# VectorE takes over the weight and token sums of a seven-product matmul

## The reference, cut to what matters

```python
x = x + gate1 * mix
h2 = rmsnorm(x, norm2_g) * (1.0 + scale2) + shift2
ffn = (jax.nn.silu(h2 @ w_ffn_gate) * (h2 @ w_ffn_up)) @ w_ffn_down
x = x + gate2 * ffn
```

## Time and profile before

| what | value |
|---|---|
| median of 3 runs | 1331.96 us (1331.69 to 1333.9) |
| the profiled execution's own time | 1333.38 us |
| its span in the profile | 1331.7 us |
| TensorE busy (matmul) | 1269.5 us, 95% |
| VectorE busy | 801.0 us, 60% |
| ScalarE busy | 488.4 us, 37% |
| GpSimd busy | 313.5 us, 24% |
| TensorE's granted clock, mean | 0.99 |

### The profile page before, as it was taken

The page is one execution under the profiler, slowest core; times in us unless marked ns, Lnnn a source line. Parts: engine busy times, 40 slices in busy tenths (PEclk is TensorE's granted clock), DMA queues, the critical chain, the costliest instruction groups (busy, mean ns, idle before and its releaser), DMA issues.

```text
span 1331.7 us, 19817 instructions
## 1 busy us (share of the span) xinstructions
PE 1269.5 (95%) x7734; PEld 1159.1 (87%) x7734; DVE 801.0 (60%) x1308; ACT 488.4 (37%) x812; POOL 313.5 (24%) x273
## 2 busy tenths in 40 slices
PE   5999999999999999998999899997999999999997
PEld 2798887799999999987788798887998899889986
DVE  4553112467566634372899654477873888558866
ACT  5352323353321222223677422344441344313434
POOL 1011000311011011111899400026400443005300
PEclk9999999999999999999899999999999999999999
DMA  9634231154344343452000224211323133222221
GB/s 312 193 111 119 63 95 48 40 159 142 112 158 148 122 110 98 128 187 94 1 1 2 81 79 174 64 32 32 95 95 95 32 95 96 95 63 63 88 88 79
DMA packets 87392, 129.56 MB, mean 97 GB/s; under 512 B 3529, under 2 KB 64450, under 8 KB 87186
## 3 DMA queue, kind: packets, MB, share of 16 engines
q1 hardware_dynamic: 76880, 95.17, 22.6%
q0 software_dynamic: 9104, 32.20, 7.9%
q10 hardware_dynamic: 1330, 1.10, 0.2%
HBM read 117.43 MB, written 4.73 MB: 92 GB/s over the span
## 4 chain that ended last, share of the span: by engine, by line
PE 74%; DVE 11%; POOL 6%; ACT 4%; issue 3%; DMA 1%; ACTq 0%; DVEq 0%
PE psum L421 30%; PE psum L458 27%; PE psum L664 10%; DVE seven_lo L694 5%; POOL probs L961 3%; POOL probs L967 3%; PE psum L407 1%; DVE hid L2158 1%; PE psum L1036 1%; PE psum L522 1%; PE psum L594 1%; DVE w_lo L390 1%; DVE partial L2188 1%; PE psum L1144 1%; DMA rows<-in_diff_subln_g 1%
## 5 line engine op out<-in xcount | busy, mean ns | idle before, releaser
L390 DVE TENSOR_TENSOR w_lo<-w_raw,w_hi 128x2048 fp32r<-128x2048 f32 x57 | 130.5, 2290 | 198.9 <-ACT w_hi L385 196.5
L385 ACT ACTIVATE w_hi<-w_raw 128x2048 fp32r<-128x2048 f32 x57 | 108.8, 1909 | 178.5 <-PE psum L458 107.6
L421 PE MATMUL psum<-h_hi,w_lo 128*128 128x320 f32 x672 | 154.6, 311 | 0.8 <-ACT y_nat L1486 0.8
L421 PE MATMUL psum<-h_hi,w_hi 128*128 128x320 f32 x672 | 153.1, 309 | 0.0
L421 PE MATMUL psum<-h_lo,w_hi 128*128 128x320 f32 x672 | 153.1, 309 | 0.0
L458 PE MATMUL psum<-w_hi,hid 128*128 128x512 f32 x440 | 135.6, 389 | 0.0
L421 PEld LDWEIGHTS psum<-h_hi,w_lo 128*128 128x128 f32 x672 | 111.8, 188 | 1.7 <-issue 1.7
L421 PEld LDWEIGHTS psum<-h_hi,w_hi 128*128 128x128 f32 x672 | 112.4, 188 | 0.0
L421 PEld LDWEIGHTS psum<-h_lo,w_hi 128*128 128x128 f32 x672 | 112.3, 188 | 0.0
L664 PE MATMUL psum<-h_hi,seven_lo 128*128 128x320 f32 x320 | 99.4, 311 | 4.4 <-DVE h_lo L2151 4.4
L684 ACT ACTIVATE seven_hi<-w_raw 128x512 fp32r<-128x512 f32 x100 | 61.9, 628 | 102.5 <-PE psum L664 70.6
(11 more groups left out here) (304 smaller groups left out, 2797.0 us busy)
## 6 DMA issues: line engine op xcount, KB each, us to landing
w_raw<-in_w_in SPq DMA_DIRECT2D x32, 1024.0 KB, 5.6
ada_b<-in_w_ada POOLq DMA_DIRECT2D x32, 512.0 KB, 4.0
w_raw<-in_w_ffn_gate SPq DMA_DIRECT2D x11, 1024.0 KB, 5.4
w_raw<-in_w_ffn_up SPq DMA_DIRECT2D x11, 1024.0 KB, 5.3
ada_a<-in_w_ada SPq DMA_DIRECT2D x8, 1024.0 KB, 13.2
w_raw<-in_w_ffn_down SPq DMA_DIRECT2D x8, 1024.0 KB, 5.1
w_raw<-in_w_ret_out SPq DMA_DIRECT2D x4, 1024.0 KB, 5.1
swapped<-qk_d POOLq DMA_DIRECT2D x32, 128.0 KB, 2.6
```

What stands on the lines that cost most here:

```text
L385: act.activation(w_hi[s][:, :, :], w_raw[s][:, :, :], ACT.Copy).then_inc(w_hi_done, 1)
L390: dve.tensor_tensor(w_lo[s][:, :, :], w_raw[s][:, :, :], w_hi[s][:, :, :].bitcast(F32), ALU.subtract).then_inc(w_lo_done, 1)
L421: last = pe.matmul(bank(4 * par + 2 * j + h, HALF), w[:, k, cs], x[:, k, h * HALF:(h + 1) * HALF], start=(k == 0 and n == 0), stop=(k == K ...
```

## The change

GpSimd has no sums any more: `token_sums` and `weight_sums` go from its queue. VectorE makes them, the weight sums in two functions, `sums_from_left` (T1 and T3) and `sums_of_four` (T2 and T4), and `token_sums` ahead of everything in `first_pair`. In `seven_unit` the order of VectorE changes: both groups of sums and the low parts of B11 and B21 come ahead of line 2188, the low part of T1 moves behind 2192, `low_of_hidden` moves from ahead of the lows to behind them, and the last two additions become one with both halves in one instruction. At the start of a par-0 unit VectorE waits for `hid_m`, its own last product. ScalarE takes `copy_first`, and the high parts of B21 and T1, ahead of `finish_unit`; in the first pair it makes three token sums' high parts between B21 and T1.

```diff
-            token_sums()
-            for third in range(3):
-                for unit in units_of(third):
-                    weight_sums(*unit)
...
@@ scalar, first_pair
-                prefill(0, (B11, B21, T1, B22), ready("up_first", 0, 0, 1))
+                prefill(0, (B11, B21), ready("up_first", 0, 0, 1))
                 for n in range(3):
                     high_of_token_sum(n)
+                prefill(0, (T1, B22), ready("up_first", 0, 0, 1))
...
@@ scalar, seven_units
                     if following:
                         act_seven(act, *following, B11)
-                    if previous:
-                        finish_unit(*previous)
                     copy_first(*unit)
                     if following:
                         act_seven(act, *following, B21)
                         act_seven(act, *following, T1)
+                    if previous:
+                        finish_unit(*previous)
+                    if following:
                         for p in (B22, T2, T4, T3):
                             act_seven(act, *following, p)
...
+            def sums_from_left(third, i, par):
+
+                n, w = seven_index(third, i, par), w_raw[par]
+                dve.wait_ge(w_landed[par], (unit_of(f"up{third}", i, par) - par) * 8 + 16)
+                if n:
+                    dve.wait_ge(seven_l, (SEVEN - 1) * (n - 1) + T1 + 1)
+                dve.tensor_tensor(t_sum[0][:, :, :], w[:, low_k, P:UC], w[:, low_k, 0:P], ALU.subtract).then_inc(seven_T, 1)
+                dve.wait_ge(seven_T, 4 * n + T1_DONE)
+                dve.tensor_tensor(w[:, low_k, P:UC], w[:, high_k, P:UC], w[:, low_k, P:UC], ALU.subtract).then_inc(seven_T, 1)
+
+            def sums_of_four(third, i, par):
+
+                n, w = seven_index(third, i, par), w_raw[par]
+                if n:
+                    dve.wait_ge(seven_l, (SEVEN - 1) * (n - 1) + T2 + 1)
+                if (i, par) == (0, 0):
+                    dve.wait_ge(mm_done, 2 * unit_of(f"up{third}", i, par) + AHEAD)
+                dve.tensor_tensor(t_sum[1][:, :, :], w[:, high_k, P:UC], t_sum[0][:, :, :], ALU.subtract).then_inc(seven_T, 1)
+                dve.wait_ge(seven_T, 4 * n + T2_DONE)
+                dve.wait_ge(seven_l, (SEVEN - 1) * n + B11 + 1)
+                dve.tensor_tensor(w[:, low_k, 0:P], w[:, high_k, 0:P], t_sum[1][:, :, :], ALU.subtract).then_inc(seven_T, 1)
...
@@ vector, first_pair
-                weights_low((0, 0, 0), (B11, B21, T1, B22))
-                for n in range(4):
+                token_sums()
+                sums_from_left(0, 0, 0)
+                weights_low((0, 0, 0), (B11, B21))
+                for n in range(3):
                     low_of_token_sum(n)
+                weights_low((0, 0, 0), (T1, B22))
+                low_of_token_sum(3)
+                sums_of_four(0, 0, 0)
                 weights_low((0, 0, 0), (T2,))
...
@@ vector, seven_unit
+                if par == 0 and HID_BASE[third] + first_tile(third, i):
+                    dve.wait_ge(hid_m, HID_BASE[third] + first_tile(third, i))
                 dve.wait_ge(seven_copy, n + 1)
                 dve.wait_ge(seven_mm, before + B21 + 1)
                 dve.tensor_tensor(out[:, 0, first_half], partial[:, :], y, ALU.add).then_inc(seven_read, 1)
-                if pending:
-                    low_of_hidden(*pending)
                 if following:
-                    weights_low(following, (B11, B21, T1))
+                    sums_from_left(*following)
+                    weights_low(following, (B11, B21))
+                    sums_of_four(*following)
...
                 if following:
-                    weights_low(following, (B22, T2))
-                else:
+                    weights_low(following, (T1, B22, T2))
+                if pending:
+                    low_of_hidden(*pending)
+                if not following:
                     dve_split(dve, unit_of(f"down{third}", 0, 0), 0)
...
-                dve.tensor_tensor(out[:, 1, second_half], partial[:, :], z, ALU.add).then_inc(freed["dve"], 1)
-                dve.tensor_tensor(out[:, 0, second_half], partial[:, :], y, ALU.add).then_inc(freed["dve"], 1)
+                dve.tensor_tensor(out[:, :, second_half], partial[:, :].unsqueeze(1).to_broadcast([P, 2, HALF]), T_tile(4 * par + 1),
+                                  ALU.add).then_inc(freed["dve"], 2)
...
@@ vector, ends of the first two thirds
-                               following=lambda: weights_low(first, (B11, B21, T1, B22)))
+                               following=lambda: (sums_from_left(*first), weights_low(first, (B11, B21, T1, B22))))
+                    sums_of_four(*first)
                     weights_low(first, (T2, T4, T3))
```

More of the change, by code:

```diff
@@ L2158, in low_of_hidden, with token_sums @@
                     dve.tensor_tensor(hid_lo[:, k, :], hid_f[:, j, :], hid_hi[:, k, :].bitcast(F32), ALU.subtract).then_inc(hid_l, 1)
+            def token_sums():
+                x11, x21 = hf2[:, low_k, first_half], hf2[:, low_k, second_half]
+                x12, x22 = hf2[:, high_k, first_half], hf2[:, high_k, second_half]
+                dve.wait_ge(n2t["h2"]["lo"], 2 * KT)
+                dve.tensor_tensor(token_sum(0), x21, x22, ALU.add).then_inc(x_sum, 1)
+                dve.wait_ge(x_sum, 1)
+                dve.tensor_tensor(token_sum(1), token_sum(0), x11, ALU.subtract).then_inc(x_sum, 1)
+                dve.tensor_tensor(token_sum(2), x11, x21, ALU.subtract).then_inc(x_sum, 1)
+                dve.wait_ge(x_sum, 2)
+                dve.tensor_tensor(token_sum(3), x12, token_sum(1), ALU.subtract).then_inc(x_sum, 1)
             def first_pair():
-                weights_low((0, 0, 0), (B11, B21, T1, B22))
-                for n in range(4):
+                token_sums()
+                sums_from_left(0, 0, 0)
+                weights_low((0, 0, 0), (B11, B21))
+                for n in range(3):
                     low_of_token_sum(n)
+                weights_low((0, 0, 0), (T1, B22))
+                low_of_token_sum(3)
+                sums_of_four(0, 0, 0)
                 weights_low((0, 0, 0), (T2,))
```

## The result

The median went from 1332.63 us (4 runs) to 1315.28 us (4 runs, 1314.67 to 1317.89): 17.35 us less, ratio 0.9873, 95% interval 0.9856 to 0.9890. Forecast were 17.3 us less and 1314.7. The profiled execution took 1314.7 us with a span of 1313.0.

The account below looks back on a forecast made before the run. TensorE, busy 95% of the span, bounds the kernel, so only its idle time can go: first pair 8.0 + steady pairs 7.0 + thirds' starts 2.2 = 17.3 us (17.2 by rounding), giving 1314.7 us; own spread 1313 to 1318.

Parts of the forecast that it names:

- 19.3 us lost: TensorE's idle time in the seven products before the change: 7.03 in steady pairs, 2.23 at thirds' starts, 10.04 in the first.
- the starts of the thirds: Second and third third: sums move into VectorE's idle time in the down stage, T3 on time; gain 2 x 1.11 = 2.23 us.
- The pairs: Steady pairs of feed-forward units fall to TensorE's 24.64 us each, since T3 no longer waits; 7.03 us go.
- the first pair: First pair of units: T3 starts at 918.2 instead of 926.17, 8.0 us go; 2.1 us of idling stay.
- Does VectorE hold?: Steady pairs with the sums on VectorE: it works 22.9 of 24.64 us, T3 has about 0.9 us to spare.
- (c): VectorE becomes the bound; kernel slower from about 1.03 us a sum, 1379 at GpSimd's 1.62; chance 0.04.
- Why was VectorE late?: Line 2188: VectorE's two-input operations were held until GpSimd's sums ended, 1.79 us for a subtraction against 0.68.
- (a): 2188 still late for T3 in steady pairs; only 10.2 and some 2 of the 7.0 us go: 1319.8; chance 0.17.
- (b): First pair cleaner: its remaining 2.1 us of idling do not appear: 1312.6; chance 0.10.
- (d): The 1.79 us are `t_sum`'s own and stay; 27.3 us a pair, 1341; chance 0.03.
- the lower bound of 5.3: First pair's smallest gain in us, if its remaining idling drops TensorE's granted clock.
- price of up to 2.7 us: Estimated cost of a clock drop after the first pair's idling: 18 matmuls at 0.147 us more each.

Follow-up runs that it names:

- e5: Changed kernel plus one unused VectorE addition of 128x448 per unit, ahead of the reads of T2: 1315.97 us.
- e6: Changed kernel plus three unused VectorE additions of 128x448 per unit, ahead of the reads of T2: 1333.26 us.
- e3: Changed kernel plus 80 unused GpSimd additions of constant 128x448 tiles, four a unit, where its weight sums had stood: 1353.97 us.
- e4: Changed kernel plus 80 GpSimd memsets of a 128x448 tile, four a unit: 1314.65 us; first of the seven products to end 408.52 us against 408.50.
- e9: Changed kernel with the 80 weight sums given back to GpSimd, all new orders, token sums on VectorE and merged addition kept: 1314.61 us.
- e11: Kernel before with only VectorE's new order in `seven_unit` (and the guard wait on `hid_m`), sums still on GpSimd: 1329.21 us.
- e10: Kernel before with only ScalarE's new order (`copy_first` and high parts of B21 and T1 ahead of `finish_unit`) and the guard wait: 1335.34 us.
- e1: Changed kernel with ScalarE's order undone, `finish_unit` again ahead of `copy_first`: 1317.13 us.

## Why the prediction was right, and where it was not

*The path.* TensorE's waits were the only thing to win, and the prediction found nearly all of them. It counted 19.3 us lost before; the lengths of the three `up` stages (85.16, 102.69 and 77.95 us, against 73.77, 98.41 and 73.77 without loss) say 19.85. Of the missing 0.55 us, 0.3 is a misreading: 1046.06 and 1203.88 in rows 4 are where pieces of the chain begin, and the first matmuls of those thirds started at 1045.90 and 1203.72, so the starts of the thirds lost 2.55 us and not 2.23. The other 0.2 lies behind the last restarts. After the change 2.2 us of loss are left up to the first T3 (first matmul at 904.50: 917.27 - 904.50 = 12.77 where 10.56 are needed), 2.07 forecast.

*The terms.* The pairs gave the 7.0 us that were forecast, the starts of the thirds 2.55 where 2.2 were forecast, the first pair 7.8 where 8.0 were, and 0.2 came from the thirds' ends: 17.6, as measured in the stretch. That the forecast of 17.3 us meets the medians' 17.35 so closely is luck in the last half microsecond: these small misses partly cancel, and the executions of either kernel spread over 2.2 and 3.2 us.

*Does VectorE hold?* It did. A sum on VectorE costs 0.61 us to the next start, 0.72 with a wait of its own; e5 and e6 show both sides of the bound that rival (c) rested on, with 1.5 us to spare per pair, not 1.7. The page's rule on semaphores (the Trainium skill, "VectorE: DVE Perf Modes", The DRAIN you can't avoid) does not fit here: 0.72 against 0.61.

*Why was VectorE late?* Here my step was incomplete. "VectorE was held until GpSimd had done" is right as mechanism (e3, e4), and I took it for the reason of the 7.0 us. e9 shows that with the new orders the lock costs TensorE nothing while VectorE's low parts are still stretched (mean 0.89 and 0.95 us). e11 and e10 show that neither order does it alone on the kernel before: `up1` becomes 1.5 us shorter with VectorE's, 1.5 us longer with ScalarE's, and 4.3 us shorter with both (e9). What decides is what stands in each queue ahead of the copy and ahead of the reads of T2. Before, about 3.3 us of stretched or movable work stood there (a held low part of T1 of 1.8 and the hidden pair's low parts of 1.5). With the sums off GpSimd, VectorE's order alone is nearly enough (e1); with them on it, ScalarE's is needed too. So VectorE's order together with either ScalarE's order or the move of the sums gives nearly the whole: I had priced the three as one sum and could not see that one was superfluous.

One part was undone in no run: e9 and e1 have the merged last addition, e10 and e11 do not. By its rows it is small: 0.82 us in the changed kernel, against 0.88 from the start of the first to the end of the second of the two before.

*The rivals.* (a) fell: no wait for `partial` in any steady pair. (b) fell for the reason given, the sums ahead of 2188. (d) is refuted by the 0.685 us of `t_sum`'s form. (c) is refuted for this change, and e6 shows where it begins.

*The clock* stayed at 1.00 through the 1.9 us of idling, so the lower bound of 5.3 did not come up. Its price of up to 2.7 us was too high for what the kernel before shows: nine matmuls 0.12 us further apart, 1.1 us.

Not tried: the orders of before with the sums on VectorE. It would price the move of the sums without any reordering, so what the headline change is worth by itself stays open.

## What to carry to other kernels

When an engine's result is needed at one date in a cycle, list what stands ahead of it in that engine's queue, and move behind it all that has a later date. Do it for every engine on the way (here ScalarE's copy and VectorE's reads), since one order alone may gain little or lose (e11, e10). Moving work off a contended engine pays only if the contention reaches the bounding engine: give the work back with the new order kept, and see (e9). Where a cycle is nearly full, sum the times between starts in the queue and test the sum with dummy operations: one that is hidden and three that are not bracket the spare time (e5, e6).

## What the runs showed of the hardware

An operation of VectorE with two SBUF inputs and an addition or subtraction of GpSimd that reads SBUF hold each other, and the one that began second is held. VectorE's operation of 128x512 then ends 0.55 us behind GpSimd's, one of 128x640 0.68 us behind it and one of 128x1280 1.35 us behind it (kernel before, e3 and e9); unheld they take 0.69, 0.82 and 1.49 us, so a held one ends behind the other by its own length less 0.14 us. GpSimd's sum of 128x512 ends 1.16 us behind VectorE's operation, and takes 1.29 us unheld. GpSimd memsets hold nothing and are not held (80 of 0.47 us changed 408.50 to 408.52). An operation with one SBUF and one PSUM input is not held (0.48 us beside both). A subtraction of 128x512 takes VectorE 0.69 us and GpSimd 1.29 us, each unheld.
